# Two weight chunks multiplied piece by piece in turn behind each norm, in a float32 transformer kernel

## The chip, the cores and the metric

One core of a Trainium2 chip runs the whole program. The metric is the time of one execution in microseconds (us), as a median of several runs; less is better.

## The reference

Two transformer blocks of two layers each, on 256 tokens with 1024 features, everything in float32. `c` is a condition vector; its product with `w_ada` gives shifts, scales and gates (the modulation).

```python
def first_block(...):
    for l in range(DEPTH):
        ada = jax.nn.silu(c) @ w_ada[l] + b_ada[l]
        sh1, sc1, g1, sh2, sc2, g2 = [a[:, None, :] for a in jnp.split(ada, 6, axis=-1)]
        h = x * (1.0 + sc1) + sh1
        ...
        x = layer_norm(DEEPNORM_ALPHA * x + (1.0 + g1) * y, ln_g[l, 0], ln_b[l, 0])
        h = x * (1.0 + sc2) + sh2
        y = swiglu(h, w_ffn_in[l], w_ffn_out[l])
        x = layer_norm(DEEPNORM_ALPHA * x + (1.0 + g2) * y, ln_g[l, 1], ln_b[l, 1])

def swiglu_half_step(x, g, mod, j, w_up, w_down):
    h = modulate(rms_norm(x, g), mod[..., j, :], mod[..., j + 1, :])
    gt, up = jnp.split(h @ w_up, 2, axis=-1)
    return x + MACARON_W * mod[..., j + 2, :] * ((jax.nn.silu(gt) * up) @ w_down)
```

`y` in the first block is an attention mixer (`mixer_ab` in layer 0, `mixer_cd` in layer 1): a product of `h` with `w_in`, attention, a product with `w_o`. The second block does a `swiglu_half_step`, an attention between the normed `x` and a normed context, and another half step, per layer. Its context of 256 tokens goes through the same weights with its own condition vector, so most of its stages work on 512 tokens and two condition vectors; the very last ones work on 256.

## The kernel before

Activations lie transposed: a tile is 128 features by 256 or 512 tokens, and a 1024-feature activation is eight tiles. A weight chunk is 1024 rows (8 k-tiles) by `CW` = 256 columns, 1 MB, and comes into one of `RAW` = 4 raw slots by SP's queue (L736). Float32 products are made of three matmuls of reduced type (`product`, L895): H_hi by weight_hi, H_lo by weight_hi, H_hi by weight_lo. So each weight is split. A chunk is cut in four pieces of two k-tiles; ScalarE writes a piece's weight_hi (L1242), VectorE its weight_lo (L683), into one of `SPLIT` = 4 split slots. The numbering of all pieces of the program, `PIECES`, gives the order. `ahead(p)` splits piece p + 4, once TensorE has used piece p (its slot), and the loops of ScalarE and VectorE call it piece by piece, in the order of the program, with their other work between.

TensorE's `features` multiplies the four pieces of a chunk one after the other into a pair of banks. There are two pairs, so group n must wait until group n-2 has been evacuated (`wait_bank`).

The stages around the change are these. A norm (on VectorE) has a statistics part and then a loop over the eight tiles: VectorE scales the tile (L1655, in the first block's layer norms also L1660), writes H_hi (L1672), ScalarE writes the modulated tile in full float32 (tmp, L1326), GpSimd subtracts to H_lo (L853), and TensorE may multiply that tile. The first weight chunk behind a norm (`ready`) waits tile by tile for it; the second finds all tiles there. There are eight norms that are followed so by `ffn_in` or `qkv`, and two modulations without norm or with a layer norm before `qkv`.

`ffn_in` has 11 steps. Step k multiplies chunk g, then chunk u; ScalarE takes silu of g's banks (L1398, L1399; the first brings a table load), VectorE multiplies by u's banks (L1690), ScalarE and GpSimd split the product for the second matrix. `qkv` goes through a list of items, one chunk each, evacuated by ScalarE's copies (L1367). `proj` has four groups m = 0 to 3 of one or three chunks, each evacuated by VectorE into X (L1713 and L1715, or L1723), and the last evacuation is what the next norm waits for.

The modulation c @ w_ada is done on VectorE, beside all this: a chunk of 512 columns by 512 rows takes a raw slot, and VectorE multiplies it by the condition in four parts for each condition vector into ada_partial (L1542, L1545), a part behind each split of the chunk that hosts it. TensorE sums over partitions (`sum_rows`), VectorE adds the bias (L1579). Such a chunk is hosted by an item of qkv, a step of ffn_in or a group of proj (`host`): SP loads it after the first weight chunk of its step.

Before, `ffn_in` hosts in steps 0 to 10 and `proj` behind it in groups 0 to 2, and `qkv` from item 0 on.

Of the kernel before, what the change touches and what calls it, by code (L numbers as in the profile page):

```python
# [31 lines left out]
P = 128  # L32
# [8 lines left out]
KC = 8  # L41
# [151 lines left out]
class Stage:  # L193


    def __init__(self, kind, *, ada=None, bias=None, bias_in=None, chunks=None, diff=None,
                 first=None, gain=None, gain_b=None, gate=None, groups=None, h_wait=None, half=None, hidden=None,
                 hi=None, host=None, items=None, koff=None, ktile=None, last_ln=None, layer=None, hosted=None,
                 mm=None, n=None, name=None, nblk=None, need=None, normed=None, o_wait=None, out=None, pairs=None,
                 q_in=None, qoff=None, qtile=None, ready=None, rmm=None, ro=None, root=None, rows=None, sums=None, scale=None,  # L200
                 shift=None, silu=None, sink=None, sq=None, steps=None, take=None, unroll=None, vblk=None,
                 vcol=None, vrow=None, vw=None, what=None, x=None, x_out=None, a32=None, halves=None, sub=None):
# [11 lines left out]
        self.halves, self.sub = halves, sub  # L214
# [47 lines left out]
def _build(nc, ctx, a, c, out):  # L262
# [402 lines left out]

    def raw_ap(n, kt, cw):
# [64 lines left out]
    def _(sp):  # L731
# [159 lines left out]
    def _(pe):  # L891
# [41 lines left out]
        def features(at, f, grp, kt_all, k_base, xh, xl, n, width=2, left=None, ready=None, hook=None):  # L933
# [3 lines left out]
            for i, pc in enumerate(ch.pieces):  # L937
                wait_split(pe, at, lambda s: f(s).pieces[i])
# [62 lines left out]
        def qkv(s):  # L1001
            for i, it in enumerate(s.items):
                ch, grp = it.chunk, it.grp
                ready = modulated(s.ready) if it is s.items[0] else None
                hook = (lambda j: qk_norm(s, i, j)) if s.layer >= 2 else None
                if it.what[0] == "forget":
# [5 lines left out]
                    continue  # L1012
                wait_bank(one, lambda _: grp)
                pair = PAIR[grp.n % 2]
# [3 lines left out]
                elif it.what[0] == "kv":  # L1018
                    part = tokens(ch, grp, s.n, P, P, lambda tt: pair[1], lambda tt: P * tt)
                    features(one, lambda _: ch, grp, KC, 0, HH, HL, s.n, 1, part, ready=ready, hook=hook)  # L1020
                else:
                    features(one, lambda _: ch, grp, KC, 0, HH, HL, it.n, ready=ready, hook=hook)
# [5 lines left out]
        def ffn_in(s):  # L1028
            def step(at, ready=None):
                wait_bank(at, lambda k: s.steps[k].gg)  # L1030
                features(at, lambda k: s.steps[k].g, s.steps[at.u].gg, KC, 0, HH, HL, s.n, ready=ready)
# [4 lines left out]
            step(At(None, 0, 1, 1), modulated(s.h_wait))  # L1036
# [194 lines left out]
    def _(act):  # L1231
# [79 lines left out]
        def modulate(s):  # L1311
# [3 lines left out]
            def tile(at):  # L1315
# [11 lines left out]
                ins.then_inc(mod_t2.sem, 1)  # L1327
            each(act, 0, 8, 2, tile)
# [21 lines left out]
        def qkv(s):  # L1350
# [3 lines left out]
            for i, it in enumerate(s.items):  # L1354
# [3 lines left out]
                for j, p in enumerate(it.chunk.pieces):  # L1358
# [25 lines left out]
        def ffn_in(s):  # L1384
# [7 lines left out]
            def step(at):  # L1392
                gg = s.steps[at.u].gg
                for i in range(KC // PIECE):
# [8 lines left out]
                for i in range(KC // PIECE):  # L1403
# [103 lines left out]
    def _(dve):  # L1507
# [43 lines left out]

        def ahead_of(at, f, host=None, hook=None):
# [76 lines left out]
        def norm(s):  # L1629
# [18 lines left out]
            def tile(at):  # L1648
# [24 lines left out]
                ins.then_inc(mod_hi.sem, 1)  # L1673
            each(dve, 0, 8, 2, tile, chain if linked else None, 2)
# [3 lines left out]
        def ffn_in(s):  # L1678
            n = s.n

            def step(at):
                ahead_of(at, lambda k: s.steps[k].g, (lambda k: s.steps[k].host) if s.steps[at.u].host else None)
                ahead_of(at, lambda k: s.steps[k].u)
# [184 lines left out]
        for s in PLAN:  # L1868
# [13 lines left out]
            elif s.kind == "qkv":  # L1882
                for i, it in enumerate(s.items):
                    if it.what[0] == "forget":
                        forget_cum()
                        continue
                    ahead_of(one, lambda _: it.chunk, (lambda _: it.host) if it.host else None,
# [39 lines left out]
```

## Time and profile before

| what | value |
|---|---|
| median of 3 runs | 2823.49 us (2822.88 to 2828.95) |
| the profiled execution | 2827.61 us |
| its span | 2825.8 us |
| TensorE busy | 2630.3 us, 93% |
| VectorE busy | 1769.0 us, 63% |
| ScalarE busy | 1086.2 us, 38% |
| GpSimd busy | 226.9 us, 8% |
| mean granted clock of TensorE | 0.959 |
| moved by DMA | 413.80 MB, mean 146 GB/s |

In the profile the engines are PE (TensorE), DVE (VectorE), ACT (ScalarE), POOL (GpSimd) and SP. An instruction's row gives its start in us from the start of the span, its duration, engine, line, operation, output and inputs with their shapes, and in brackets the idle time of the engine before it and what ended that. "x4" counts like instructions in one row. The clock is the share of TensorE's full speed that was granted.

### The profile page before, as it was taken

To read this page: it belongs to the slowest core of one execution; us is meant where nothing else is said; L and a number is where in the kernel's file an instruction comes from. 1 tells how busy PE (TensorE), PEld (TensorE's weight loads), DVE (VectorE), ACT (ScalarE), POOL (GpSimd) and SP (SyncE) were. 2 spreads that over 40 slices of the span, in tenths; PEclk is the share of its full clock that TensorE was granted. 3 is DMA by queue.
4 is the path that set the end of the run, shared out by engine and by line. 5 is a ranking of instruction groups with operands and counts; after the bars stand their busy time and mean duration, and the time that the engine had idled before them with its cause. 6 is when DMAs were issued, how large, how long until landed. Compare 5 with 4: busy or idle time off the path is not lost. (4 is left out here: it accounts for less than half of the span.)

```text
span 2825.8 us, 40791 instructions
## 1 busy us (share of the span) xinstructions
PE 2630.3 (93%) x15939; PEld 2259.5 (80%) x15939; DVE 1769.0 (63%) x3184; ACT 1086.2 (38%) x2068; POOL 226.9 (8%) x170
## 2 busy tenths in 40 slices
PE   4768999999998999999999999999999999989999
PEld 4748998968998688887765778888788888777999
DVE  6567776657777656545759675554555533668754
ACT  2243544444443433323338233322333322446553
POOL 2000100001000211101000021110111100100110
PEclk8868999868999999999999999999999999999999
DMA  8924874914765244332620334433244433522653
GB/s 295 261 89 139 265 250 151 271 46 152 238 230 186 75 135 148 131 123 90 164 88 2 120 100 154 135 127 112 91 148 145 138 124 116 147 75 84 215 176 124
DMA packets 354873, 413.80 MB, mean 146 GB/s; under 512 B 24737, under 2 KB 291914, under 8 KB 354618
## 3 DMA queue, kind: packets, MB, share of 16 engines
q1 hardware_dynamic: 352496, 404.13, 44.8%
q0 software_dynamic: 832, 4.65, 0.5%
q8 instruction: 126, 2.06, 0.3%
q10 hardware_dynamic: 1354, 2.43, 0.2%
q14 instruction: 65, 0.53, 0.1%
HBM read 409.56 MB, written 5.27 MB: 147 GB/s over the span
## 5 line engine op out<-in xcount | busy, mean ns | idle before, releaser
L683 DVE TENSOR_TENSOR weight_lo<-raw_weights,weight_hi 128x512 fp32r<-128x512 f32 x1024 | 774.6, 763 | 886.0 <-ACT weight_hi L1242 873.9
L1242 ACT ACTIVATE weight_hi<-raw_weights 128x512 fp32r<-128x512 f32 x1024 | 635.6, 631 | 1326.7 <-PE bank L895 1203.9
L895 PE MATMUL bank<-H_hi,weight_hi 128*128 128x256 f32 (+1 forms) x2832 | 967.6, 342 | 71.3 <-POOL H_lo L853 46.3
L895 PE MATMUL bank<-H_lo,weight_hi 128*128 128x256 f32 (+1 forms) x2832 | 947.8, 335 | 0.0
L895 PE MATMUL bank<-H_hi,weight_lo 128*128 128x256 f32 (+1 forms) x2832 | 947.4, 335 | 0.0
L895 PEld LDWEIGHTS bank<-H_hi,weight_hi 128*128 128x128 f32 x2832 | 548.9, 194 | 156.9 <-issue 75.9
L895 PEld LDWEIGHTS bank<-H_hi,weight_lo 128*128 128x128 f32 x2832 | 549.5, 194 | 50.6
L895 PEld LDWEIGHTS bank<-H_lo,weight_hi 128*128 128x128 f32 x2832 | 550.2, 194 | 47.7 <-issue 1.0
L1545 DVE SCALAR_TENSOR_TENSOR ada_partial<-raw_weights,silu_c,ada_partial 128x512 f32<-128x512 f32 x616 | 441.1, 743 | 1.7 <-issue 0.4
L895 PE MATMUL bank<-hidden_hi,weight_hi 128*128 128x256 f32 (+1 forms) x1056 | 358.7, 340 | 3.2 <-DVE weight_lo L683 3.2
L895 PE MATMUL bank<-hidden_hi,weight_lo 128*128 128x256 f32 (+1 forms) x1056 | 354.9, 336 | 0.0
L895 PE MATMUL bank<-hidden_lo,weight_hi 128*128 128x256 f32 (+1 forms) x1056 | 354.8, 336 | 0.0
L895 PEld LDWEIGHTS bank<-hidden_hi,weight_hi 128*128 128x128 f32 x1056 | 200.4, 190 | 25.5 <-DVE weight_lo L683 3.6
L895 PEld LDWEIGHTS bank<-hidden_lo,weight_hi 128*128 128x128 f32 x1056 | 200.4, 190 | 21.8 <-issue 1.4
L895 PEld LDWEIGHTS bank<-hidden_hi,weight_lo 128*128 128x128 f32 x1056 | 200.4, 190 | 20.8
L853 POOL TENSOR_TENSOR H_lo<-tmp,H_hi 128x256 fp32r<-128x256 f32 (+1 forms) x80 | 92.2, 1154 | 1464.6 <-ACT tmp L1326 1425.9
L863 POOL TENSOR_TENSOR hidden_lo<-tmp,hidden_hi 128x1024 fp32r<-128x1024 f32 (+1 forms) x66 | 121.6, 1843 | 1022.1 <-ACT hidden_hi L1390 1022.1
L1158 PEld LDWEIGHTS bank<-ident,probs 128*128 128x128 f32 x404 | 48.2, 154 | 70.7 <-issue 66.7
L895 PEld LDWEIGHTS bank<-ones,ada_partial 128*128 128x128 f32 x704 | 89.5, 199 | 17.1 <-DVEq L1550 15.1
L1390 ACT ACTIVATE hidden_hi<-tmp 128x1024 fp32r<-128x1024 f32 (+1 forms) x66 | 56.0, 849 | 120.7 <-DVE tmp L1690 120.7
L895 PE MATMUL bank<-ones,ada_partial 128*128 128x1 f32 x704 | 86.1, 249 | 14.9 <-DVEq L1550 14.9
L895 PE MATMUL bank<-weight_hi,H_hi 128*128 128x256 f32 (+1 forms) x320 | 93.3, 291 | 6.4 <-DVE weight_lo L683 6.4
(172 smaller groups left out, 2169.4 us busy)
## 6 DMA issues: line engine op xcount, KB each, us to landing
raw_weights<-in_w_ada_dram SPq DMA_DIRECT2D x120, 1024.0 KB, 5.3
raw_weights<-in_w_ffn_up_dram SPq DMA_DIRECT2D x88, 1024.0 KB, 5.5
raw_weights<-in_w_ffn_in_dram SPq DMA_DIRECT2D x44, 1024.0 KB, 5.9
raw_weights<-in_w_ffn_down_dram SPq DMA_DIRECT2D x32, 1024.0 KB, 5.2
raw_weights<-in_w_in_dram SPq DMA_DIRECT2D x18, 1024.0 KB, 6.0
raw_weights<-in_w_ffn_out_dram SPq DMA_DIRECT2D x16, 1024.0 KB, 7.7
raw_weights<-in_w_in_ab_dram SPq DMA_DIRECT2D x12, 1024.0 KB, 10.0
raw_weights<-in_w_in_cd_dram SPq DMA_DIRECT2D x12, 1024.0 KB, 8.2
```

Of the source, the lines that this page charges most:

```text
L683: eng.tensor_tensor(WL[:, p.g % SPLIT, 0:p.kt * CW].rearrange("p (t n) -> p t n", n=CW), raw_ap(ch.n, ch.kt, CW)[:, p.k0:p.k0 + p.kt, :], ...
L853: pool.tensor_tensor(HL[:, bass.ds(t, 1), 0:s.n], T2[:, par:par + 1, 0:s.n], HH[:, bass.ds(t, 1), 0:s.n].bitcast(F32), ALU.subtract).then_ ...
L863: pool.tensor_tensor(AL[:, bass.ds(t, 2), 0:s.n], T2[:, :, 0:s.n], AH[:, bass.ds(t, 2), 0:s.n].bitcast(F32), ALU.subtract).then_inc(act_re ...
L895: return pe.matmul(o, w, x, start=start, stop=stop, skip_group_check=True)
L1158: ins = pe.transpose(bank[:, col:col + P], PR[:, 2 * (h.n % 2) + hh, P * b:P * b + P], ident[:, :])
L1242: act.activation(WH[:, p.g % SPLIT, 0:p.kt * CW].rearrange("p (t n) -> p t n", n=CW), raw_ap(ch.n, ch.kt, CW)[:, p.k0:p.k0 + p.kt, :], ACT ...
L1390: act.activation(AH[:, bass.ds(t, 2), 0:n], T2[:, :, 0:n], ACT.Copy).then_inc(act_hi.sem, 1)
L1545: ins = dve.scalar_tensor_tensor(out=acc, in0=w[:, k, :], scalar=SILU_C[:, i:i + 1], in1=acc, op0=ALU.mult, op1=ALU.add)
```

## The change

Behind a norm or modulation the two first chunks (`lead`: g and u of step 0, or the chunks of items 0 and 1) are multiplied in the order g0 u0 g1 u1 g2 u2 g3 u3, and their pieces are renumbered so. The first four splits that `ahead` makes for them (the third and fourth pieces of both) are put into the norm's loop over tiles, behind tiles 3, 4, 5 and 6, on ScalarE and on VectorE; the other four come at the start of the stage. Both chunks are evacuated after all four. Step 0 and item 0 host no modulation: ffn_in hosts in steps 1 to 10 and proj in groups 0 to 3, qkv from item 1 on. SP loads g and u of step 0 one behind the other. In the second block's qkv TensorE also waits for the squares of the q and k norm (`qn_sq`) at each later item.

```diff
-            a1 = ada_chunk() if host and len(ADA) < sum(ADA_CHUNKS) else None
+            a1 = ada_chunk() if s and host and len(ADA) < sum(ADA_CHUNKS) else None
...
-            groups.append(Rows(chunks=cs, host=ada_chunk() if steps[-1].host and m < 3 else None,
+            groups.append(Rows(chunks=cs, host=ada_chunk() if steps[-1].host else None,
...
-                host = ada_chunk() if len(st.items) < hosted else None
+                host = ada_chunk() if 0 < len(st.items) <= hosted else None
...
+    for s, after in zip(PLAN, PLAN[1:]):
+        if after.kind in ("ffn_in", "qkv") and s.kind in ("mod", "ln", "rms"):
+            s.lead = (after.steps[0].g, after.steps[0].u) if after.kind == "ffn_in" else \
+                (after.items[0].chunk, after.items[1].chunk)
+            at = s.lead[0].pieces[0].g
+            PIECES[at:at + 8] = [c.pieces[i] for i in range(4) for c in s.lead]
+    for k, p in enumerate(PIECES):
+        p.g = k
+    def lead_split(s, t, split_next):
+        if s.lead and t >= 3 and t < 7:
+            split_next(s.lead[t % 2 ^ 1].pieces[(t - 3) // 2])
...
         def ffn_in(s):
             def step(at):
                 load(at, lambda k: s.steps[k].g)
+                if at.u == 0:
+                    load(at, lambda k: s.steps[k].u)
                 if s.steps[at.u].host:
                     load(at, lambda k: s.steps[k].host)
-                load(at, lambda k: s.steps[k].u)
+                if at.u:
+                    load(at, lambda k: s.steps[k].u)
...
         def ffn_in(s):
-            def step(at, ready=None):
+            def first(at, ready):
+                st = s.steps[at.u]
                 wait_bank(at, lambda k: s.steps[k].gg)
-                features(at, lambda k: s.steps[k].g, s.steps[at.u].gg, KC, 0, HH, HL, s.n, ready=ready)
+                wait_bank(at, lambda k: s.steps[k].ug)
+                for k in range(KC // PIECE):
+                    features(at, lambda k: s.steps[k].g, st.gg, KC, 0, HH, HL, s.n, ready=ready, only=k)
+                    features(at, lambda k: s.steps[k].u, st.ug, KC, 0, HH, HL, s.n, only=k)
+                if st.host:
+                    ada(at, lambda k: s.steps[k].host)
...
             def step(at):
                 gg = s.steps[at.u].gg
-                for i in range(KC // PIECE):
+                if at.u == 0:
+                    for i in (2, 3):
+                        ahead(at, lambda k: s.steps[k].g.pieces[i], split, late)
+                        ahead(at, lambda k: s.steps[k].u.pieces[i], split, late)
+                for i in range(KC // PIECE) if at.u else ():
                     ahead(at, lambda k: s.steps[k].g.pieces[i], split, late)
...
+        def lead_rest(first, second, host):
+            for i in (2, 3):
+                for ch in (first, second):
+                    ahead(one, lambda _: ch.pieces[i], split, late)
+                    if host:
+                        ada(one, lambda _: host, 2 * i - 4 + (ch is second), 4)
```

ScalarE's instructions from the norm's loop to step 1's splits, at the first norm of the second block, before (L1326 writes a modulated tile for 256 tokens, two for a tile of 512; L1242 a split, L1398 and L1399 the silus):

```order
L1326 ACTIVATE tmp2<-tmp1,ada2,gain_scale 128x256 x16
L1242 ACTIVATE weight_hi<-raw_weights 128x512 x4
L1398 ACT_TABLE_LOAD
L1398 ACTIVATE tmp1<-bank0 128x512
L1399 ACTIVATE tmp1<-bank1 128x512
L1242 ACTIVATE weight_hi<-raw_weights 128x512 x4
L1390 ACTIVATE hidden_hi_49<-tmp2 128x1024
```

and the same place in the changed program (L1368, L1284, L1448, L1449 and L1436 are the same instructions):

```order
L1368 ACTIVATE tmp2<-tmp1,ada2,gain_scale 128x256 x8
L1284 ACTIVATE weight_hi<-raw_weights 128x512
L1368 ACTIVATE tmp2<-tmp1,ada2,gain_scale 128x256 x2
...
L1284 ACTIVATE weight_hi<-raw_weights 128x512 x4
L1448 ACT_TABLE_LOAD
L1448 ACTIVATE tmp1<-bank0 128x512
L1449 ACTIVATE tmp1<-bank1 128x512
L1436 ACTIVATE hidden_hi_49<-tmp2 128x1024
L1284 ACTIVATE weight_hi<-raw_weights 128x512 x4
```

Four splits have moved into the loop, and the table load and the silus now stand behind the last split of the eight of both chunks.

VectorE's instructions in the last groups of `proj` ahead of place 3 (layer 1's qkv), before:

```order
L1545 SCALAR_TENSOR_TENSOR ada_partial<-raw_weights,silu_c,ada_partial 128x512 x2
L1713 TENSOR_SCALAR tmp2<-bank0,ada0 128x256
L1713 TENSOR_SCALAR tmp2<-bank1,ada0 128x256
L1715 SCALAR_TENSOR_TENSOR X<-X,tmp2 128x2x256
L683 TENSOR_TENSOR weight_lo<-raw_weights,weight_hi 128x512 x11
L1713 TENSOR_SCALAR tmp2<-bank2,ada0 128x256
L1713 TENSOR_SCALAR tmp2<-bank3,ada0 128x256
L1715 SCALAR_TENSOR_TENSOR X<-X,tmp2 128x2x256
```

and in the changed program (L698 is the split, L1595 the modulation, L1775 and L1777 the evacuation, L1637 the bias):

```order
L1777 SCALAR_TENSOR_TENSOR X<-X,tmp2 128x2x256
L698 TENSOR_TENSOR weight_lo<-raw_weights,weight_hi 128x512 x9
L1637 TENSOR_TENSOR ada1<-bank7,b_ada_cols 128x4
L1595 SCALAR_TENSOR_TENSOR ada_partial<-raw_weights,silu_c,ada_partial 128x512
L698 TENSOR_TENSOR weight_lo<-raw_weights,weight_hi 128x512
L1595 SCALAR_TENSOR_TENSOR ada_partial<-raw_weights,silu_c,ada_partial 128x512
L698 TENSOR_TENSOR weight_lo<-raw_weights,weight_hi 128x512
L1595 SCALAR_TENSOR_TENSOR ada_partial<-raw_weights,silu_c,ada_partial 128x512 x2
L1775 TENSOR_SCALAR tmp2<-bank2,ada0 128x256
L1775 TENSOR_SCALAR tmp2<-bank3,ada0 128x256
L1777 SCALAR_TENSOR_TENSOR X<-X,tmp2 128x2x256
```

The last group, which had splits only, now has four modulation products among the last three splits and ahead of the evacuation.

SP's queue around the step from the product with w_o to ffn_in in layer 0, before:

```order
L736 DMA raw_weights<-in_w_o_dram 128x8x256
L736 DMA raw_weights<-in_w_ada_dram 128x4x512
L736 DMA raw_weights<-in_w_ffn_in_dram 128x8x256
L736 DMA raw_weights<-in_w_ada_dram 128x4x512
L736 DMA raw_weights<-in_w_ffn_in_dram 128x8x256 x2
```

and in the changed program:

```order
L751 DMA raw_weights<-in_w_o_dram 128x8x256
L751 DMA raw_weights<-in_w_ada_dram 128x4x512
L751 DMA raw_weights<-in_w_ffn_in_dram 128x8x256 x3
L751 DMA raw_weights<-in_w_ada_dram 128x4x512
```

The modulation chunk between g and u of step 0 is gone, and step 1's g comes right behind them.

## Rows read from the trace of the kernel before

**Rows 1.** busy time per engine (page); granted clock in 40 slices of the span (page)

```profile
PE 2630.3 (93%) x15939; PEld 2259.5 (80%) x15939; DVE 1769.0 (63%) x3184; ACT 1086.2 (38%) x2068; POOL 226.9 (8%) x170
...
PEclk8868999868999999999999999999999999999999
```

**Rows 2.** waits of PE: us in total, times, longest us

```profile
PE bank L895 <- POOL H_lo L853: 46.3, 50, 4.0
PE bank L895 <- DVE weight_lo L683: 29.4, 25, 8.7
```

**Rows 3.** timeline of POOL, place 7: start us, us, instruction, idle before and releaser

```profile
1625.33 1.27 POOL L853 TENSOR_TENSOR H_lo<-tmp,H_hi 128x512 fp32r<-128x512 f32 x1 [279.55 <-ACT tmp L1326]
...
1640.43 1.29 POOL L853 TENSOR_TENSOR H_lo<-tmp,H_hi 128x512 fp32r<-128x512 f32 x1 [0.55 <-DVE H_hi L1672]
```

**Rows 4.** timeline of PE, place 7, first matmul

```profile
1626.74 0.47 PE L895 MATMUL bank<-H_hi,weight_hi 128*128 128x512 f32 x1 [2.76 <-POOL H_lo L853]
```

**Rows 5.** timeline of ACT, place 7

```profile
1643.53 0.64 ACT L1242 ACTIVATE weight_hi<-raw_weights 128x512 fp32r<-128x512 f32 x1 [1.97 <-PE bank L895]
1644.19 1.28 ACT L1398 ACT_TABLE_LOAD   x1
1645.48 0.60 ACT L1398 ACTIVATE tmp<-bank 128x512 f32<-128x512 f32 x1
...
1654.41 0.63 ACT L1242 ACTIVATE weight_hi<-raw_weights 128x512 fp32r<-128x512 f32 x1 [2.09 <-PE bank L895]
```

**Rows 6.** windows of PE, places 7 and 5: us, busy (count), clock, DMA share, GB/s

```profile
1624.00:1640.00 16.00, 9.84 (x36) 1.00 0.00 1
934.00:950.00 16.00, 11.49 (x38) 0.89 0.00 0
```

**Rows 7.** timeline of DVE, place 7, a split alone

```profile
1643.59 0.68 DVE L683 TENSOR_TENSOR weight_lo<-raw_weights,weight_hi 128x512 fp32r<-128x512 f32 x1
```

**Rows 8.** timelines of POOL (first row) and ACT, place 2

```profile
271.68 0.74 POOL L853 TENSOR_TENSOR H_lo<-tmp,H_hi 128x256 fp32r<-128x256 f32 x1 [0.23 <-DVE H_hi L1672]
...
275.49 0.39 ACT L1398 ACTIVATE tmp<-bank 128x256 f32<-128x256 f32 x1
...
280.18 0.63 ACT L1242 ACTIVATE weight_hi<-raw_weights 128x512 fp32r<-128x512 f32 x1 [0.81 <-PE bank L895]
```

**Rows 9.** windows of PE, places 3 and 4

```profile
482.70:503.00 20.30, 18.87 (x78) 0.50 0.38 107
673.80:690.70 16.90, 15.92 (x64) 0.50 0.02 3
```

**Rows 10.** timeline of DVE, last two groups of proj before place 6; first row before place 3

```profile
450.32 1.53 DVE L1545 SCALAR_TENSOR_TENSOR ada_partial<-raw_weights,silu_c,ada_partial 128x512 f32<-128x512 f32 x2
...
1286.26 0.69 DVE L683 TENSOR_TENSOR weight_lo<-raw_weights,weight_hi 128x512 fp32r<-128x512 f32 x1 [0.70 <-ACT weight_hi L1242]
1286.87 2.74 DVE L1545 SCALAR_TENSOR_TENSOR ada_partial<-raw_weights,silu_c,ada_partial 128x512 f32<-128x512 f32 x4
1289.75 1.66 DVE L1723 SCALAR_TENSOR_TENSOR X<-bank,gain_scale,X 128x256 f32<-128x256 f32 x4
...
1317.94 0.69 DVE L683 TENSOR_TENSOR weight_lo<-raw_weights,weight_hi 128x512 fp32r<-128x512 f32 x1 [2.02 <-ACT weight_hi L1242]
1318.55 1.65 DVE L1723 SCALAR_TENSOR_TENSOR X<-bank,gain_scale,X 128x256 f32<-128x256 f32 x4
```

**Rows 11.** issues: KB each, us to landing (page); timeline of SP, before place 2

```profile
raw_weights<-in_w_ffn_in_dram SPq DMA_DIRECT2D x44, 1024.0 KB, 5.9
...
236.94 0.37 SPq L736 DMA_DIRECT2D raw_weights<-in_w_ada_dram  x1
```

**Rows 12.** timeline of DVE, last evacuation before place 2

```profile
244.12 0.87 DVE L1713 TENSOR_SCALAR tmp<-bank,ada 128x256 f32<-128x256 f32 x2
```

**Rows 13.** timeline of ACT, place 1

```profile
82.30 2.19 ACT L1242 ACTIVATE weight_hi<-raw_weights 128x512 fp32r<-128x512 f32 x4 [12.47 <-DMA raw_weights<-in_w_in_ab_dram]
```

**Rows 14.** timeline of SP, place 1

```profile
65.19 0.37 SPq L736 DMA_DIRECT2D raw_weights<-in_w_ada_dram  x1
```

More of the change, by code:

```diff
@@ L213, in __init__ @@
         self.vw, self.what, self.x, self.x_out, self.a32 = vw, what, x, x_out, a32
-        self.halves, self.sub = halves, sub
+        self.halves, self.sub, self.lead = halves, sub, lead
 class Group:
@@ L931, in wait_bank, with features @@
                 pe.wait_ge(before(at.u).tally.sem, at(lambda s: before(s).done))
-        def features(at, f, grp, kt_all, k_base, xh, xl, n, width=2, left=None, ready=None, hook=None):
+        def features(at, f, grp, kt_all, k_base, xh, xl, n, width=2, left=None, ready=None, hook=None, only=None):
             ch = f(at.u)
             for i, pc in enumerate(ch.pieces):
+                if only is not None and i != only:
+                    continue
                 wait_split(pe, at, lambda s: f(s).pieces[i])
@@ L1012, in qkv @@
                     continue
+                pair = PAIR[grp.n % 2]
+                if i < 2:
+                    wait_bank(one, lambda _: grp)
+                    if i == 0:
+                        continue
+                    both = s.items[0:2]
+                    for k in range(KC // PIECE):
+                        for m, b in enumerate(both):
+                            part = tokens(b.chunk, b.grp, s.n, P, P, lambda tt: PAIR[b.grp.n % 2][1], lambda tt: P * tt) \
+                                if b.what[0] == "kv" else None
+                            features(one, lambda _: b.chunk, b.grp, KC, 0, HH, HL, b.n, 1 if part else 2, part,
+                                     ready=modulated(s.ready) if m == 0 else None, only=k)
+                    if it.host:
+                        ada(one, lambda _: it.host)
+                    continue
                 wait_bank(one, lambda _: grp)
-                pair = PAIR[grp.n % 2]
+                if s.layer >= 2:
+                    pe.wait_ge(qn_sq.sem, s.sq + sum(len(item_tiles(b)) for b in s.items[:i - 1]))
                 if it.what[0] == "v":
@@ L1017, in qkv @@
                     features(one, lambda _: ch, grp, KC, 0, HH, HL, s.n, 0, part, hook=hook)
-                elif it.what[0] == "kv":
-                    part = tokens(ch, grp, s.n, P, P, lambda tt: pair[1], lambda tt: P * tt)
-                    features(one, lambda _: ch, grp, KC, 0, HH, HL, s.n, 1, part, ready=ready, hook=hook)
                 else:
-                    features(one, lambda _: ch, grp, KC, 0, HH, HL, it.n, ready=ready, hook=hook)
+                    features(one, lambda _: ch, grp, KC, 0, HH, HL, it.n, hook=hook)
                 if it.host:
@@ L1028, in ffn_in, with step @@
         def ffn_in(s):
-            def step(at, ready=None):
+            def first(at, ready):
+                st = s.steps[at.u]
                 wait_bank(at, lambda k: s.steps[k].gg)
-                features(at, lambda k: s.steps[k].g, s.steps[at.u].gg, KC, 0, HH, HL, s.n, ready=ready)
+                wait_bank(at, lambda k: s.steps[k].ug)
+                for k in range(KC // PIECE):
+                    features(at, lambda k: s.steps[k].g, st.gg, KC, 0, HH, HL, s.n, ready=ready, only=k)
+                    features(at, lambda k: s.steps[k].u, st.ug, KC, 0, HH, HL, s.n, only=k)
+                if st.host:
+                    ada(at, lambda k: s.steps[k].host)
+            def step(at):
+                wait_bank(at, lambda k: s.steps[k].gg)
+                features(at, lambda k: s.steps[k].g, s.steps[at.u].gg, KC, 0, HH, HL, s.n)
                 if s.steps[at.u].host:
@@ L1035, in step @@
                 features(at, lambda k: s.steps[k].u, s.steps[at.u].ug, KC, 0, HH, HL, s.n)
-            step(At(None, 0, 1, 1), modulated(s.h_wait))
+            first(At(None, 0, 1, 1), modulated(s.h_wait))
             each(pe, 1, 11, unroll(s), step)
@@ L1327, in tile @@
                 ins.then_inc(mod_t2.sem, 1)
+                lead_split(s, t, lambda p: ahead(one, lambda _: p, split, late))
             each(act, 0, 8, 2, tile)
@@ L1357, in qkv @@
                     continue
-                for j, p in enumerate(it.chunk.pieces):
+                if i == 0:
+                    for p in [b.chunk.pieces[j] for j in (2, 3) for b in s.items[0:2]]:
+                        ahead(one, lambda _: p, split, late)
+                for j, p in enumerate(it.chunk.pieces) if i > 1 else ():
                     ahead(one, lambda _: p, split, late)
@@ L1402, in step @@
                 act.sem_inc(ev_act.sem, 1)
-                for i in range(KC // PIECE):
+                for i in range(KC // PIECE) if at.u else ():
                     ahead(at, lambda k: s.steps[k].u.pieces[i], split, late)
@@ L1673, in tile @@
                 ins.then_inc(mod_hi.sem, 1)
+                lead_split(s, t, lambda p: ahead(one, lambda _: p, split, late))
             each(dve, 0, 8, 2, tile, chain if linked else None, 2)
@@ L1886, in _ @@
                         continue
+                    if i == 1:
+                        lead_rest(s.items[0].chunk, it.chunk, it.host)
+                    if i < 2:
+                        continue
                     ahead_of(one, lambda _: it.chunk, (lambda _: it.host) if it.host else None,
```

10 lines of the change are left out of this document (6 added, 4 removed).

## Prediction

> **What bounds the kernel now.** I read the page first: TensorE is busy 93% of the span, VectorE 63%, ScalarE 38%, GpSimd 8%, so what counts is the 195 us in which TensorE is idle, and the stretches in which its granted clock is below 1 [rows 1]. Next the waits of TensorE: 46.3 us in 50 waits end with GpSimd's H_lo, the last product of a norm's tile, and 29.4 us in 25 waits with VectorE's weight_lo [rows 2]. There are ten places where a norm or modulation is followed by two weight chunks. I number them 1 to 10 in order of time: 1 the first layer's modulation before qkv, 3 layer 1's qkv, 6 and 9 the second block's qkv, the others ffn_in; 5 to 9 multiply 512 tokens, the rest 256.
>
> Place 7 shows the pattern. GpSimd starts eight H_lo from 1625.33 to 1640.43, one in 2.16 us [rows 3]; TensorE starts at 1626.74 after 2.76 us of idle time [rows 4]. Without waits TensorE does a piece of two tiles in 2.72 us (ScalarE's split at 1654.41 takes 0.63 us after 2.09 idle, in which it waits for TensorE to be done with a piece [rows 5]), so a tile is 1.36 us of work for a norm that gives one in 2.16, and TensorE waits for nearly each. The second chunk begins only when the first is done, and its last piece is done at 1654.4. A chunk is four pieces, 10.88 us of TensorE, and the pair 21.8, against 27.67 us from first matmul to end. Between the two chunks ScalarE does the split at 1643.53, a table load of 1.28 us and two silus, and all of that lies beside the second chunk's matmuls.
>
> **a) TensorE's waits in the norm.** Multiplied piece by piece, a tile of H feeds 2.72 us of TensorE, more than the norm's 2.16. What is left is one wait for tile 1 (0.85 us) and 21.8 us of work: 22.6 for 27.7, so -5.1 us at places 6 and 7, where the clock stays at 1 [rows 6]. At 5, 8 and 9 it falls to 0.5 for 3.4 us behind the first matmul (5 is the second row of [rows 6]: 16 us with a mean of 0.89 are 3.5 us at 0.5). TensorE was waiting for the norm then, so it cost nothing; now it costs 1.7 us: -3.4 each. The 512-wide places give 2x5.1 + 3x3.4 = -20.4.
> With 256 tokens a tile feeds only 1.44 us, and the loops of VectorE are the limit. The four splits put into VectorE's loop add 4 x 0.65 = 2.6 us (a split is 0.68 us and overlaps a little [rows 7]). At place 2 the last H_lo ends at 272.4 and the pair at 280.1, where ScalarE's split at 280.18 waits for TensorE [rows 8]. Now: 272.4 + 2.6 + 2.2 (the last tile of one chunk 0.72, the last piece of the other 1.44) = 277.2, or -2.9. By the same sum 10 gives -2.0. At 4 the clock is at 0.5 for 17 us (the second row of [rows 9]), and work of 11.5 us at half speed becomes the limit: -2.4. At 3 it is low for 20 us, and the same sum gives -1.4. Together -8.7.
>
> **b) The new wait.** Group 2 (step 1) may start only when ScalarE has evacuated group 0. That silu used to lie beside chunk u. Now it stands behind the last of four splits, which waits for the last piece of the pair, and the order of ScalarE confirms it. TensorE stands still for the split 0.64, the load 1.28 and the silus 1.1 (0.60 each, with 0.1 of overlap) [rows 5], with 0.1 for the semaphores: 3.1 us at 5, 7 and 8. With 256 tokens (0.39 a silu [rows 8], 0.66 for both) it is 2.65 at 2, 4 and 10. At 6 some 1.1, since TensorE has the modulation's row sums to do meanwhile; at 9 a split, two copies and two squares, 2.8. At 1 and 3 copies only, inside f. Sum 9.3 + 7.95 + 1.1 + 2.8 = +21.2. A weighed rule: the load at 1644.19 ends at 1645.47 and the silu starts at 1645.48, and the load starts 0.02 us behind the split, so 1.28 us is all that the switch costs here. The Trainium skill (page ScalarE: Activation LUTs, section What ACT_TABLE_LOAD costs) adds a drain of about 1380 ns to each switch to another set; by it six of these waits would be 1.38 us longer, 8.3 in all. The trace disagrees, and I leave it out of the sum.
>
> **c) The clock behind the new wait.** Seven of these waits are 2.6 us or longer. Of eight idle stretches of 2.6 to 2.8 us ahead of a norm's first matmul, six were followed by a fall to 0.5 and two (6 and 7) by none [rows 4, 6, 9]. A short fall lasts 3.4 us and costs 1.7. So 7 x 0.75 x 1.7 = +8.9. Bounds: 0, and +15 more if two of them last as at 4 (17 us, costing 8.5).
>
> **d) Modulation in proj's last group.** The chunk not hosted by step 0 goes to group m = 3. VectorE's four products of it (2.74 us) stand between the last split and the evacuation: at 1286.26 a split, at 1289.75 the evacuation, 3.5 us later, for m = 2; for m = 3 without modulation 0.6 us (1317.94 to 1318.55) [rows 10]. The norm behind m = 3 waits for this X, and nothing covers it. So +2.9 with two condition vectors (before 5, 6 and 8), and +1.7 with one (450.32: 1.53 us and gaps) before 3 and 9: 8.7 + 3.4 = +12.1. What step 0 is freed of lay beside TensorE and gives nothing.
>
> **e) The later second chunk.** At places 2 and 10 SP now sends g, u, modulation where it sent g, modulation, u. There is one raw slot fewer for the modulation chunk, and u's must wait until VectorE has used the chunk before. At 2, the load behind g was issued at 236.94, the modulation's then, u's now, and the last evacuation of proj was at 244.12 [rows 11, 12]. A load of this tensor takes 5.9 us (the page's row in [rows 11]), so u lands at 243, and the four splits and VectorE's modulation behind it push the evacuation to 247.4. I take +3.3 there and, 10 lying alike, +2.5, together +5.8, with bounds 0 and 8.
>
> **f) Place 1** is bound by transfers. ScalarE waits 12.47 us for a weight at 82.30 [rows 13]. SP issues no weight before 65.19 [rows 14], since the mask and bias transfers in its queue wait for the modulated H. With pair-wise work that comes up to 4.8 us later, while each weight stands one chunk (3.4 us) earlier. I take +4, between -3 and +8. g) The first ffn_in of layer 1 loses a step bound by VectorE: 25 waits for weight_lo are 1.2 us each, so -1.2.
>
> **Sum**: -20.4 - 8.7 + 21.2 + 8.9 + 12.1 + 5.8 + 4 - 1.2 = +21.7. Profiled time 2827.6 + 21.7 = 2849.3; that run lies 4.1 above the median of the three, 2823.5, so I say **2845**.
>
> **Rivals.** (1) ScalarE's evacuation is not in TensorE's path: it starts while the last piece is still being multiplied. Then b and c fall away, -30.1, and the kernel gets faster, 2815. It decides from where the silu starts before the pair ends; against it speaks the order, in which the load stands behind the last split. Chance 0.07. (2) The moved modulation and the later chunk are hidden: d and e fall away, 2827, no change. For it: VectorE has 37% idle; against it: the 3.5 us of [rows 10] stand right ahead of the evacuation. 0.13. (3) The clock stays low at two of the new waits for 17 us, as at 3 and 4: +15, 2860. 0.14. (4) No new fall of the clock, and none that costs at 5, 8 and 9: -8.9 - 5.1, 2831. 0.11. (5) The switch of tables holds ScalarE for longer than the load, once TensorE waits behind it: at most as long again, 6 x 1.28 = +7.7, 2853. Against it: no gap around the load at 1644.19. 0.04. The Trainium skill's page on ScalarE, named in b, gives that drain as about 1380 ns. (6) The change does not do what it says: the in-loop splits wait for TensorE and hold up the norm, so that a is 0: 2874. 0.03.
>
> **The numbers.** A measurement of this kernel can tell about 0.2%, 5.6 us, from no change: 2818 to 2829. The forecast has 0.48. Faster: rival 1 and 0.02 of the forecast's own spread, 0.09. Same: rival 2 and 0.03 of rival 4, 0.16. Slower 0.75. Of the range, 2827 takes in half of rival 2, 2864 takes in 3; rivals 1, 6 and the tails are left out.
>
> **What would show it.** Right: behind each pair a TensorE idle time of 2.6 to 3.1 us at L895 released by ScalarE's tmp, at six places, with the table load inside it; GpSimd's waits down from 46.3 to about 25; the evacuation 3.5 us behind the last split in m = 3. I would be wrong if that idle time is missing, if the pair at place 7 takes more than 24 us, or if the granted clock stays at 1 everywhere behind a new wait.

## The result and the profile after

The changed kernel takes 2884.08 us (2879.33 to 2886.25, 4 runs) against 2826.22 us for the kernel before (4 runs): a ratio of 1.0195, with a 95% interval of 1.0171 to 1.0220. It is 55 us slower by the ratio, 58 by the medians. Slower was forecast; the size was not, since 2884 lies 20 us above the top of the range, and the profiled execution gained 56.1 us (2827.61 to 2883.76) where the sum gave 21.7.

| | before | after |
|---|---|---|
| profiled execution | 2827.61 us | 2883.76 us |
| span | 2825.8 us | 2881.7 us |
| TensorE busy | 2630.3 us | 2634.1 us |
| mean granted clock | 0.959 | 0.956 |

The page and the waits of TensorE in the changed kernel, to be laid beside [rows 1, 2]:

```profile
PE 2634.1 (91%) x15939; PEld 2270.1 (79%) x15939; DVE 1759.4 (61%) x3184; ACT 1079.8 (37%) x2068; POOL 219.3 (8%) x170
...
PEclk8878999888999899999999999999999999999999
```

```profile
PE bank L913 <- POOL H_lo L871: 47.5, 32, 4.0
PE bank L913 <- DVE weight_lo L698: 35.2, 26, 13.0
PE bank L913 <- ACT tmp L1334: 20.0, 11, 5.8
...
PE bank L913 <- DVEq L1789: 18.9, 4, 7.8
PE bank L913 <- ACTq L1452: 18.3, 6, 3.5
```

The work of TensorE is the same, so the 56 us are idle time and clock. Three of the rows are what was announced: the squares of the norm (L1334, 13.0 us before) and the evacuation (DVEq L1789, 8.8 us before) are late, and there is a new wait for ScalarE's evacuation (ACTq L1452). But the first row should have shrunk to some 25 us, and it did not shrink at all. The pair was to save just that.

Where the time came, by the start of GpSimd's first H_lo at each place: it lies 1.4 us later than before at place 1, then 14.9, 25.4, 25.8, 34.7, 42.0, 39.0, 43.9, 48.4 and 50.1 us later at places 2 to 10, and the end 55.9. Only the stretch from 6 to 7 won time.

Place 7 shows what happened in the norm. GpSimd, in the changed kernel, tiles 3 to 7:

```profile
1670.53 1.27 POOL L871 TENSOR_TENSOR H_lo<-tmp,H_hi 128x512 fp32r<-128x512 f32 x1 [0.55 <-DVE H_hi L1730]
1674.60 1.30 POOL L871 TENSOR_TENSOR H_lo<-tmp,H_hi 128x512 fp32r<-128x512 f32 x1 [2.79 <-ACT tmp L1368]
1678.42 1.29 POOL L871 TENSOR_TENSOR H_lo<-tmp,H_hi 128x512 fp32r<-128x512 f32 x1 [2.53 <-ACT tmp L1368]
1682.52 1.29 POOL L871 TENSOR_TENSOR H_lo<-tmp,H_hi 128x512 fp32r<-128x512 f32 x1 [2.81 <-ACT tmp L1368]
1686.34 1.26 POOL L871 TENSOR_TENSOR H_lo<-tmp,H_hi 128x512 fp32r<-128x512 f32 x1 [2.53 <-ACT tmp L1368]
```

A tile with a split comes after 3.95 us (15.81 us for four), where [rows 3] had one in 2.16. ScalarE and then VectorE in the same stretch:

```profile
1677.18 1.09 ACT L1368 ACTIVATE tmp<-tmp,ada,gain_scale 128x256 f32<-128x256 f32 x2 [2.18 <-DVE tmp L1713]
1678.19 0.61 ACT L1284 ACTIVATE weight_hi<-raw_weights 128x512 fp32r<-128x512 f32 x1
```

```profile
1676.36 0.68 DVE L1713 TENSOR_TENSOR tmp<-X,rstd 128x512 f32<-128x512 f32 x1
1677.08 0.74 DVE L1730 TENSOR_SCALAR H_hi<-tmp,gain_scale,ada 128x256 fp32r<-128x256 f32 x2
1678.83 1.43 DVE L698 TENSOR_TENSOR weight_lo<-raw_weights,weight_hi 128x512 fp32r<-128x512 f32 x1 [1.02 <-ACT weight_hi L1284]
1680.18 0.68 DVE L1713 TENSOR_TENSOR tmp<-X,rstd 128x512 f32<-128x512 f32 x1
```

Read them together: VectorE scales the tile until 1677.04, ScalarE writes the modulated tile until 1678.27 and the weight's high part until 1678.80, VectorE idles 1.02 us for that, then needs 1.43 us for the low part (0.68 alone, [rows 7]) beside GpSimd's H_lo, and only then scales the next tile. The loop has become a chain through both engines. That the chain is at fault, and not VectorE's own work, shows in its busy time from the start of tile 3's H_lo to that of tile 7's. In the changed kernel, and then in e1 below, which takes the wait away (us, busy and count, clock, DMA share, GB/s):

```profile
1670.53:1686.34 15.81, 10.30 (x16) 0.96 0.25 77
```

```profile
1656.26:1667.98 11.72, 11.56 (x16) 0.95 0.15 50
```

The same 16 instructions were busy for 1.3 us more in e1, and VectorE's idle time fell from 5.5 us to 0.2.

And behind the pair, TensorE at place 7, and its wait:

```profile
1687.65 0.50 PE L913 MATMUL bank<-H_hi,weight_hi 128*128 128x512 f32 x1 [1.15 <-POOL H_lo L871]
...
1695.25 0.50 PE L913 MATMUL bank<-H_hi,weight_hi 128*128 128x512 f32 x1 [3.22 <-ACTq L1452]
```

```profile
1692.12 0.63 ACT L1284 ACTIVATE weight_hi<-raw_weights 128x512 fp32r<-128x512 f32 x1 [2.09 <-PE bank L913]
1692.77 1.28 ACT L1448 ACT_TABLE_LOAD   x1
1694.07 0.60 ACT L1448 ACTIVATE tmp<-bank 128x512 f32<-128x512 f32 x1
1694.56 0.59 ACT L1449 ACTIVATE tmp<-bank 128x512 f32<-128x512 f32 x1
```

This wait is term b as it was forecast: split, load, two silus, 3.22 us for 3.1. The pair itself took 26.3 us, where the prediction had named more than 24 as a sign that it is wrong.

At place 1, SP and ScalarE in the changed kernel ([rows 13, 14] answer to them):

```profile
67.85 0.34 SPq L801 DMA_DIRECT2D causal<-const_neg_causal_dram  x1
68.29 0.38 SPq L751 DMA_DIRECT2D raw_weights<-in_w_ada_dram  x1
68.76 0.46 SPq L751 DMA_DIRECT2D raw_weights<-in_w_in_ab_dram  x1
69.27 10.62 SPq L801 DMA_DIRECT2D bias<-t_skew  x1
```

```profile
89.04 1.15 ACT L1284 ACTIVATE weight_hi<-raw_weights 128x512 fp32r<-128x512 f32 x2 [17.00 <-DMA raw_weights<-in_w_in_ab_dram]
```

The mask, which waits for the whole modulated H, leaves at 67.85, where it left at 60.45; ScalarE waits 17.00 us for a weight where it waited 12.47. Place 3 has the same queue. There ScalarE's next splits wait 9.24 us for a weight that SP sent behind the mask, and the copies that TensorE needs stand behind them:

```profile
532.49 2.19 ACT L1284 ACTIVATE weight_hi<-raw_weights 128x512 fp32r<-128x512 f32 x4 [9.24 <-DMA raw_weights<-in_w_in_cd_dram]
534.59 1.18 ACT L1413 ACTIVATE q<-bank 128x256 f32<-128x256 f32 x4
```

### The profile page after: what moved, and what is told of

Read it like the earlier page. It is cut to its first block and busy times, and to the rows that moved or that the text cites. A ratio compares the mean times of both kernels' runs of the same rounds, so it can differ in the third digit from the quotient of the medians.

```text
span 2881.7 us, 40791 instructions
## 1 busy us (share of the span) xinstructions
PE 2634.1 (91%) x15939; PEld 2270.1 (79%) x15939; DVE 1759.4 (61%) x3184; ACT 1079.8 (37%) x2068; POOL 219.3 (8%) x170
## 5 line engine op out<-in xcount | busy, mean ns | idle before, releaser
L698 DVE TENSOR_TENSOR weight_lo<-raw_weights,weight_hi 128x512 fp32r<-128x512 f32 x1024 | 787.4, 776 | 943.2 <-ACT weight_hi L1284 932.4
L1284 ACT ACTIVATE weight_hi<-raw_weights 128x512 fp32r<-128x512 f32 x1024 | 634.4, 629 | 1346.0 <-PE bank L913 1190.8
L1595 DVE SCALAR_TENSOR_TENSOR ada_partial<-raw_weights,silu_c,ada_partial 128x512 f32<-128x512 f32 x616 | 441.4, 744 | 1.7 <-issue 0.4
L871 POOL TENSOR_TENSOR H_lo<-tmp,H_hi 128x256 fp32r<-128x256 f32 (+1 forms) x80 | 85.0, 1063 | 1540.5 <-ACT tmp L1368 1506.8
L913 PEld LDWEIGHTS bank<-ones,ada_partial 128*128 128x128 f32 x704 | 88.3, 197 | 18.2 <-DVEq L1600 15.2
L1436 ACT ACTIVATE hidden_hi<-tmp 128x1024 fp32r<-128x1024 f32 (+1 forms) x66 | 55.8, 846 | 117.6 <-DVE tmp L1752 117.6
L913 PE MATMUL bank<-ones,ada_partial 128*128 128x1 f32 x704 | 85.1, 247 | 14.9 <-DVEq L1600 14.9
```

The lines of the kernel that those rows point to most:

```text
L698: eng.tensor_tensor(WL[:, p.g % SPLIT, 0:p.kt * CW].rearrange("p (t n) -> p t n", n=CW), raw_ap(ch.n, ch.kt, CW)[:, p.k0:p.k0 + p.kt, :], ...
L871: pool.tensor_tensor(HL[:, bass.ds(t, 1), 0:s.n], T2[:, par:par + 1, 0:s.n], HH[:, bass.ds(t, 1), 0:s.n].bitcast(F32), ALU.subtract).then_ ...
L913: return pe.matmul(o, w, x, start=start, stop=stop, skip_group_check=True)
L1284: act.activation(WH[:, p.g % SPLIT, 0:p.kt * CW].rearrange("p (t n) -> p t n", n=CW), raw_ap(ch.n, ch.kt, CW)[:, p.k0:p.k0 + p.kt, :], ACT ...
L1436: act.activation(AH[:, bass.ds(t, 2), 0:n], T2[:, :, 0:n], ACT.Copy).then_inc(act_hi.sem, 1)
L1595: ins = dve.scalar_tensor_tensor(out=acc, in0=w[:, k, :], scalar=SILU_C[:, i:i + 1], in1=acc, op0=ALU.mult, op1=ALU.add)
```

## The experiments

The kernel before ran beside each group of them, on the same chip; ratios are to it, with 95% intervals.

**e1: VectorE's in-loop splits one tile later.**

```diff
+    def lead_split_low(s, t, split_next):
+        lead_split(s, t - 1, split_next)
...
                 ins.then_inc(mod_hi.sem, 1)
-                lead_split(s, t, lambda p: ahead(one, lambda _: p, split, late))
+                lead_split_low(s, t, lambda p: ahead(one, lambda _: p, split, late))
```

> The changed kernel (2884) with one edit: in the norm's loop VectorE's weight_lo splits stand one tile later (behind tiles 4 to 7) than ScalarE's weight_hi splits (behind 3 to 6). Theory A (the loop is a chain: VectorE's scaling, ScalarE's modulated tile, ScalarE's split, VectorE's split, next tile, 3.8 to 4.1 us a tile at place 7 where I had reckoned 2.9): the period falls to about 3.0, the pair at place 7 from 26.3 to about 23.5 us, over nine places 15 to 20 us less, 2866. Rival B (VectorE's own work and GpSimd's port share make the period, or TensorE is the limit anyway): the period stays above 3.6, at most 5 us less, 2880.

Measured: 2865.1 us, ratio 1.0101 (1.0044 to 1.0159), 19 us below the changed kernel by the medians and 0.9% by the ratios. The same loop of VectorE at place 7, in e1:

```profile
1661.38 0.68 DVE L702 TENSOR_TENSOR weight_lo<-raw_weights,weight_hi 128x512 fp32r<-128x512 f32 x1
1661.98 0.68 DVE L1717 TENSOR_TENSOR tmp<-X,rstd 128x512 f32<-128x512 f32 x1
1662.71 1.59 DVE L1734 TENSOR_SCALAR H_hi<-tmp,gain_scale,ada 128x256 fp32r<-128x256 f32 x2
1664.22 0.68 DVE L702 TENSOR_TENSOR weight_lo<-raw_weights,weight_hi 128x512 fp32r<-128x512 f32 x1
```

No idle time is left in the rows, and H_lo starts at 1656.26 for tile 3 and 1667.98 for tile 7: 2.93 us a tile. The pair at place 7 goes from 26.3 to 24.9 us (23.5 was expected), at place 8 from 25.8 to 22.9. Theory A: the splits cost so much because VectorE waited for ScalarE in the same tile, and not because of their own time.

**e2: the first chunk evacuated ahead of the last split.**

```diff
                 if at.u == 0:
-                    for i in (2, 3):
-                        ahead(at, lambda k: s.steps[k].g.pieces[i], split, late)
-                        ahead(at, lambda k: s.steps[k].u.pieces[i], split, late)
+                    ahead(at, lambda k: s.steps[k].g.pieces[2], split, late)
+                    ahead(at, lambda k: s.steps[k].u.pieces[2], split, late)
+                    ahead(at, lambda k: s.steps[k].g.pieces[3], split, late)
...
                 act.sem_inc(ev_act.sem, 1)
-                for i in range(KC // PIECE) if at.u else ():
+                for i in range(KC // PIECE) if at.u else (3,):
```

and the same in qkv.

> The changed kernel with one edit: behind a pair ScalarE evacuates the first chunk's group between the seventh and the eighth of the splits, as soon as the first chunk's last piece is done, so that it lies beside the second chunk's last piece. Theory A (the new idle time of TensorE is split + table load + evacuation behind the pair's last piece, 2.8 us with 256 tokens, 3.2 to 3.5 with 512): the eight idle times fall below 1.3 us, -18 to -22, and up to 8 more where the clock no longer falls behind them: 2858. Rival B (the wait only moves to the late split of the fourth piece or to VectorE's evacuation): less than 6 us, 2879.

Measured: 2861.1 us, ratio 1.0098 (1.0072 to 1.0125). TensorE at the end of the pair at place 7, in e2:

```profile
1683.88 0.50 PE L913 MATMUL bank<-H_hi,weight_hi 128*128 128x512 f32 x1 [0.48 <-ACTq L1454]
```

0.48 us are left of 3.22; over 0.9 us are left only 1.36 at places 4 and 10 and 1.66 at place 3. Theory A: 23 us came back by the medians (0.97% by the ratios), where it had 26.

**e3 and e4: where the modulation is hosted.** e3 is the changed kernel with

```diff
+            if s == 0:
+                a1 = ada_chunk() if host and len(ADA) < sum(ADA_CHUNKS) else None
...
-            groups.append(Rows(chunks=cs, host=ada_chunk() if steps[-1].host else None,
+            groups.append(Rows(chunks=cs, host=ada_chunk() if steps[-1].host and m < 3 else None,
```

and e4 the kernel before with the opposite edit.

> The changed kernel, but ffn_in hosts modulation in step 0 again (behind both chunks) and proj not in its last group. Theory A (term d: the modulation ahead of the last evacuation delays the norm's statistics by 2.1, 4.8, 2.9, 1.1 and 0.8 us, 11.7 in all by the waits of the trace): 2872. Rival B (step 0's modulation now delays the splits of the pair, and eats it up): within 4 us of 2884.

> The kernel before, with only the moving of ffn_in's modulation from step 0 to the last group of proj. Theory A (term d stands by itself, +12, step 0 gives nothing back): 2838. Rival B (in the old order VectorE has slack there, and layer 1's first step gets shorter): 2824 to 2829.

Measured: e3 2876.0 us, ratio 1.0142 (1.0098 to 1.0187); e4 2837.4 us, ratio 1.0015 (0.9993 to 1.0036). In both traces the waits before the statistics are as forecast. The last evacuation in the changed kernel before place 6 stands behind its modulation, 3.5 us behind the split, as m = 2 did in [rows 10]:

```profile
1355.67 0.69 DVE L698 TENSOR_TENSOR weight_lo<-raw_weights,weight_hi 128x512 fp32r<-128x512 f32 x1 [0.70 <-ACT weight_hi L1284]
1356.28 2.73 DVE L1595 SCALAR_TENSOR_TENSOR ada_partial<-raw_weights,silu_c,ada_partial 128x512 f32<-128x512 f32 x4
1359.16 1.66 DVE L1785 SCALAR_TENSOR_TENSOR X<-bank,gain_scale,X 128x256 f32<-128x256 f32 x4
```

The wait of TensorE there is 3.81 us in the changed kernel and in e4, and 0.93 in e3 and in the kernel before. As a whole e3 gave back 8 us by the medians and 15 by the ratios, give or take some 14: theory A's 12 fits, but the times alone can't tell it from 4. e4 cost 5 us, give or take 6, and the 2838 of theory A was met only because the kernel before ran at 2832.5 beside it. Its trace has 10.4 us of these waits more than the kernel before, and pays 2.7 back: the waits for weight_lo fall from 29.4 to 26.7 us, and the one of 2.03 us ahead of place 5 is gone.

**e5 and e6: place 1.** e5 lets SP send the mask and bias one item later in the first two layers (`first = 3` for `2`). e6 takes the pair away at places 1 and 3:

```diff
-        if after.kind in ("ffn_in", "qkv") and s.kind in ("mod", "ln", "rms"):
+        if (after.kind == "ffn_in" or after.kind == "qkv" and after.layer >= 2) and s.kind in ("mod", "ln", "rms"):
```

with the old loops for these two stages, and their modulation hosted from item 0 again.

> The changed kernel, but in the first two layers' qkv SP sends the mask and bias transfers, which wait for the whole modulated H, one item later. Theory A (at place 1 the queue stood from 50.8 to 67.85 for them, where before it stood to 60.45, and with it the weights: TensorE's wait went from 8.7 to 13.0 us): that wait falls under 9 us, and about 5 to 8 us of the 13.6 that came between places 1 and 2 return: 2877. Rival B (the raw slots of the pair come free late, and the queue would wait for them anyway): the wait stays at 11 us or more, less than 2 us.

> The changed kernel with the old order at places 1 and 3 (the qkv of layers 0 and 1, hosting from item 0 again); the other eight places keep the pair. Theory A (both places lose: 10 us at 1 through the queue, 3.6 us of a new wait for two copies at 3): first H_lo of place 2 back from 274.6 to about 264.5, in all -12 to -16: 2870. Rival B (what is lost at 1 comes from the late second chunk and the moved modulation ahead of 2): less than 5 us, 2880.

Measured: e5 2867.7 us (2859.4 to 2884.4), ratio 1.0154 (1.0120 to 1.0188); e6 2862.4 us, ratio 1.0124 (1.0098 to 1.0150). In e5 the wait at place 1 is 7.67 us instead of 12.99, but place 2 comes only 3.4 us sooner, where 5 to 8 were expected: later weights wait in turn for the bias transfers. The median is 16 us lower all the same, and the trace can't say by what, for the profiled execution was the slowest of the four and ends where the changed kernel's does. At place 3 the new wait of 3.62 us is gone in e5, though the copies still stand behind all the splits:

```profile
523.86 0.63 ACT L1285 ACTIVATE weight_hi<-raw_weights 128x512 fp32r<-128x512 f32 x1 [1.92 <-PE bank L914]
524.39 1.19 ACT L1414 ACTIVATE q<-bank 128x256 f32<-128x256 f32 x4
```

So that wait came of the late weight. In e6, place 2 starts at 263.05 instead of 274.64, so the pair at 1 cost 10 us or more. e6 changes both places at once; that 3 was a loss as well rests on its wait of 3.62 us, against 2.3 us that the pair was shorter there. From 3 to 4, e6 took 182.3 us and the changed kernel 190.9, but the kernel before, which has no pair either, 190.5.

**e7 and e8: the edits together.** e1, e2 and e3, and on top a silu of one column behind the norm's root, so that the table load is done while VectorE computes the reciprocal; e8 has e6's edit too.

```diff
+    WARM = sb("warm", [P, 1])
     WH = sb("weight_hi", [P, SPLIT, PIECE * CW], F32R)
...
+            if getattr(s, "warm", False):
+                act.activation(WARM[:, :], EPS[:, 0:1], ACT.Silu)
```

> The changed kernel with four edits together: VectorE's in-loop splits one tile later, the first chunk's evacuation ahead of the last split, ffn_in's modulation hosted as before, and a silu of one column behind the norm's root, so that the table load lies in the wait for the reciprocal. Theory A (the causes add: -19, -22, -8, and -1.4 at three places for the load): 2830. Rival B (they overlap: with a faster norm TensorE is fed sooner, and the splits of the pair or VectorE's hosting become the limit): 2845 or more.

> The same four edits, and no pair at places 1 and 3. Theory A (all causes found, and they add): about 2816 to 2820, so 6 to 10 us faster than the kernel before; of the 29 us that the pair was to bring, the rest goes to in-loop splits and the pair's own splits. Rival B: no better than the kernel before, 2826 to 2840, as the pair's gain is eaten by falls of the clock that a busier TensorE feels.

Measured: e7 2844.0 us, ratio 1.0063 (1.0041 to 1.0085); e8 2828.9 us, ratio 1.0020 (1.0002 to 1.0037). e7 lies 14 us above theory A, and e8 9 to 13 us, where rival B had it. e8's trace says why, in a stage where nobody waits. TensorE from 1000 to 1200, in the kernel before and in e8 (us, busy and count, clock, DMA share, GB/s):

```profile
1000.00:1200.00 200.00, 200.00 (x916) 1.00 0.44 141
```

```profile
1000.00:1200.00 200.00, 200.00 (x893) 1.00 0.40 131
```

The same loop, the same clock, no idle time, and 2.5% fewer matmuls. The only edit that reaches this stage is the new tile, which moved the addresses of all behind it. From 1050 to 1200, the kernels of this case without an added tile did 688 or 696 matmuls (ten of them), those with one 670 or 678 (four).

**e9, e10, e11, e12: the address, and the table load.** e9 is e8 with the silu written into an unused column (`LAM[:, 7:8]`) and no new tile. e10 and e12 are the kernel before with only `sb("unused", [P, 1])` or `sb("unused", [P, 16])` ahead of weight_hi. e11 is e9 without the silu of one column.

> As e8_comb_no_pair_1_3, but the silu of one column writes into an unused column of an existing tile, where e7 and e8 had a new tile of 4 bytes a partition laid ahead of weight_hi, which moved the address of everything behind it. In e8 TensorE did 893 matmuls in the 200 us from 1000 on at full clock, without a wait, where the kernel before did 916. Theory A (the shifted addresses cost TensorE 2.2 to 2.7% in every stage; the four edits were right): 916 again, and 2785 to 2800 us, 1% or more faster than before. Rival B (the rate belongs to the chip or the moment): 893 again and 2829.

> The kernel before with nothing but an unused tile of 4 bytes a partition ahead of weight_hi. Theory A (shifted addresses): about 893 matmuls in 200 us at full clock, the 512-wide matmul from 394 to 400 ns, and 2860 to 2880 us. Rival B: no change, 2824.

> As e9_comb_no_shift, without the silu of one column: the table load is back between the first chunk's last piece and its evacuation. Theory A (1.28 us of load and 1.1 of silus at 512 tokens fit in the 2.72 us of the second chunk's last piece; at 256 tokens 1.28 + 0.66 + 0.63 do not fit in 1.44, 1.4 us are left at 2, 4 and 10): 2 to 6 us more than e9. Rival B (a switch of tables holds ScalarE longer than its load): 1.3 us more at all six places, 8 to 10 us more than e9.

> The kernel before with an unused tile of 64 bytes a partition ahead of weight_hi, in place of the 4 bytes of e10. Theory A (it is the address modulo some power of two up to 64 that costs, not the layout as such): 916 matmuls in the 200 us from 1000 on, as before, and 2825 to 2831 us. Rival B (any move of what lies behind costs): 895, and 2850 us or more.

| | us | ratio | interval |
|---|---|---|---|
| e9 | 2803.9 | 0.9910 | 0.9875 to 0.9946 |
| e10 | 2854.2 | 1.0086 | 1.0055 to 1.0117 |
| e11 | 2810.0 | 0.9929 | 0.9901 to 0.9956 |
| e12 | 2850.4 | 1.0063 | 1.0038 to 1.0089 |

e9 is faster than both kernels: 0.9%, 25 us, below the one before, though its theory A had 2785 to 2800 and at least 1%. Its rate is 916 again, and e10's 895, with 2854 us where 2860 to 2880 were expected:

```profile
1000.00:1200.00 200.00, 200.00 (x916) 1.00 0.42 136
```

```profile
1000.00:1200.00 200.00, 200.00 (x895) 1.00 0.42 136
```

So the edits of e8 were good ones behind a bad address: e8 and e9 differ by the tile alone, and by 1.1%. e11 lies 0.2% above e9, inside both intervals, so its time does not decide. Its trace has a wait behind the pair of 1.36 us at place 10, 0.58 at 2 and 4, 0.51 at 7 and 8 and none at 5, 3.5 us in all: less than theory A's 1.4 at three places, and far from rival B's 1.3 more at all six. e12's theory A failed: 64 bytes cost as well.

```profile
300.00:450.00 150.00, 150.00 (x1270) 1.00 0.77 255
1000.00:1200.00 200.00, 200.00 (x893) 1.00 0.42 136
```

## Why the prediction was wrong, step by step

**a, what the pair saves (-29.1 us): this step failed.** From the first matmul's start to the last one's end: place 2 went from 19.5 to 21.3 us, 3 (with row sums in both) from 23.9 to 21.6, 4 from 22.7 to 20.4, 5 from 29.4 to 25.8, 6 from 34.7 to 28.3, 7 from 27.6 to 26.3, 8 from 27.6 to 25.8, 9 from 33.0 to 28.3, 10 from 14.2 to 15.5. At 2, 4, 5 and 6 the row sums of the modulation stood inside the pair before, 5.8 us in all, and are now done elsewhere. Without them the sum is -13.4. With 512 tokens the term set 2.72 us of matmuls against a norm of 2.16 us a tile, as if no split stood in the loop. With 256 it took a split for its own time on VectorE, 0.65 us. Nowhere did it ask whom VectorE's split waits for. It waits for ScalarE's of the same tile, which stands behind that tile's 1.1 us of modulation. That makes 3.95 us a tile for 2.16 (2.8 with a split's own time), more than the 2.72 that TensorE needs, and with 256 tokens a norm of 18.2 us for 12.7 where 15.3 was reckoned. e1 took that wait away and the period fell to 2.93: of the 1.8 us more a tile, 1.0 was the wait and 0.8 the split. Rival 6 named the neighbourhood, but another wait (for TensorE), and with a chance of 0.03.

**b, the new wait (+21.2): right.** 2.79 us at 2, 4 and 10, 3.22 at 5 and 7, 3.50 at 8, 1.04 at 6, 2.77 at 9: 22.1. e2 removed it with the edit that its mechanism asks for. Left out was place 3, of which I had said "copies only, inside f", which deals with place 1 alone. There are 3.62 us, which e5 shows to be the queue's, and 1.32 at 1.

The weighed rule was rightly left out. The load at 1692.77 ends at 1694.05 and the silu starts at 1694.07, now with TensorE waiting for it; in e9 the load follows the root at once:

```profile
1606.83 0.69 ACT L1363 ACTIVATE rstd<-bank,eps 128x512 f32<-128x512 f32 x1 [0.32 <-PE bank L924]
1607.53 1.28 ACT L1369 ACT_TABLE_LOAD   x1
1608.83 0.20 ACT L1369 ACTIVATE lam<-eps 128x1 f32<-128x1 f32 x1
```

The Trainium skill (page ScalarE: Activation LUTs, section What ACT_TABLE_LOAD costs) adds about 1380 ns of drain to a switch; no gap around any load in these rows shows one.

**c, the clock (+8.9): right in kind.** Behind the new waits the clock fell at 2, 5, 7, 8 and 10; at 4 it was at 0.5 already, and at 9 it did not fall. Five in seven is what 0.75 stood for. From the mean clocks and spans, TensorE was at half speed for 232 us before ((1 - 0.959) x 2 x 2825.8) and 254 after: 22 us more, which cost up to 11. The mean clock of the kernel before runs from 0.953 to 0.966 over the executions on record, so this total by itself is not clear of noise. Not right were some places behind the norms' first matmuls: at 7, where I counted on a clock of 1, it fell, and at 8 and 9, where I charged a fall, there was none. Place 7 behind the first matmul, place 9 there, and place 7 behind the new wait:

```profile
1664.00:1680.00 16.00, 14.31 (x51) 0.79 0.00 0
2461.00:2477.00 16.00, 15.01 (x89) 1.00 0.00 1
1695.25:1699.25 4.00, 4.00 (x11) 0.57 0.68 250
```

**d, modulation in the last group (+12.1): right in its waits**, 2.1, 4.8, 2.9, 1.1 and 0.8 us before places 3, 5, 6, 8 and 9, 11.7 in all, though distributed otherwise. e3 removed the waits and returned 8 us by the medians.

**e, the late second chunk (+5.8): right.** 7.76 us of wait before place 2 for 4.51, and before place 10 two waits for squares of 1.17 and 1.82 us for 0.30 and 0.33: 5.6 in all. At 2 the trace shows the way: ScalarE's splits of the second chunk wait 4.75 us for its load, to 254.10, VectorE waits 3.00 us for them, and the evacuation stands behind. It wasn't tried by itself; e9 still has 7.38 us there.

**f, place 1 (+4, with +8 as its upper bound): failed.** The wait for the statistics before 2 starts 11.4 us later, 1.4 of which were there at the start. I had seen that SP's queue waits for H, named up to 4.8 us of delay against 3.4 us that the earlier order of the weights might make good, and taken 4. H was complete 7.4 us later, and nothing was made good. **g (-1.2)** was one wait of 2.0 us less.

Together: -13.4 + 22.1 + 3.6 + 11 + 11.7 + 5.6 + 10 + 1.4 - 2 = 50.0 of the 56.1 us. The terms are not quite apart: within the pairs TensorE was at half speed for 51 us before and 39 after, so 6 of a's 13.4 us are the clock's, and outside the pairs the clock cost up to 17 us and not 11. That is as much as the 6 us left over, but an upper bound, from one execution of each. Of the 34 us that the sum missed, a holds 16, f 6, place 3 another 4, and the clock outside the pairs up to 8. The errors of a, f and place 3 have one root: in-loop splits that stretch the norm, and with it all who wait for its end.

## What to carry to other kernels

When work is put into a loop that two engines run in step, write down for each new instruction whose result it waits for and what that engine does first; staggering the second engine by one iteration cost nothing here and gave back 0.9%. When two products are interleaved, evacuate the first as soon as its own last piece is done, not when the pair is. And after an edit that adds a tile, compare the matmuls per 200 us in a stage that the edit does not touch.

## What the runs showed of the hardware

An unused tile of 4 bytes a partition ahead of weight_hi made TensorE slower by 2.3% in the 512-wide stages at full clock (916 to 895 matmuls in 200 us; over the whole run, the mean H_hi matmul of 512 columns went from 398 to 405 ns), and the kernel by 0.9%. 64 bytes cost as much there (893) and 0.6% in all. So it is not the remainder by 64 bytes alone. In a 256-wide stage (300 to 450 us) both tiles made it faster: 1265 matmuls with 4 bytes and 1270 with 64, for 1249 before (1264 to 1270 in the four kernels with an added tile, 1245 to 1255 in the ten without). Where the two differ is the 512-wide matmul of the hidden tiles: 394 ns before and with 64 bytes, 401 with 4. Which two tiles must lie how to one another stays open, and so does whether the layout of the kernel before is the best one.
